# Pair-wise LayerNorm roots, later routing and re-ranked finishing in a two-layer decoder trunk with a gMLP mixer and two MoE stages

## The reference, cut to what matters

```python
for i in range(DEPTH):                                   # DEPTH = 2
    sh_m, sc_m, gt_m, sh_f, sc_f, gt_f = jnp.split(c_act @ ada_w[i] + ada_b[i], 6)
    h = x * (1 + sc_m) + sh_m
    y = sliding_window_attention(h) if i == 0 else chunked_spatial_gating(h)
    x = layer_norm(DEEPNORM_ALPHA * x + (1 + gt_m) * y, post_ln_g[i, 0], post_ln_b[i, 0])
    h = x * (1 + sc_f) + sh_f
    y = hierarchical_moe(h)      # 4 groups x 8 experts, 1 group, 2 experts of it for a token
    x = layer_norm(DEEPNORM_ALPHA * x + (1 + gt_f) * y, post_ln_g[i, 1], post_ln_b[i, 1])

def chunked_spatial_gating(h):                           # chunks of 128 tokens, width 2048
    u, v = jnp.split(gelu(h @ w_in + b_in), 2, axis=-1)
    v = layer_norm(v, sgu_ln_g, sgu_ln_b)
    mixed = einsum(tril(w_s), v) + b_s                   # over the 128 positions of the chunk
    return (u * mixed) @ w_out + b_out
```

## Time and profile before

| | |
|---|---|
| median of 3 runs | 2102.83 us (2079.18, 2102.83, 2133.82) |
| profiled execution | 2081.33 us, span 2080.0 us on core 2, the slowest |
| cores 0 to 3 | 2069.3, 2074.8, 2080.0, 2067.6 us |
| cores 4 to 7 | 2011.6, 2039.3, 2048.1, 2032.3 us |
| TensorE / VectorE / ScalarE / POOL busy | 62 / 54 / 33 / 26 % of the span |
| DMA queues q0 / q1 | 62.6 / 18.2 % of the 16 engines' time |

### The profile page before, as it was taken

One profiled execution on the slowest core, in us unless ns is written; L12 is line 12 of the kernel. 1 busy time (PEld: TensorE's weight loads), 2 busy tenths in 40 slices (PEclk: granted clock), 3 DMA queues, 4 the chain that ended last, 5 costly groups with the idle time before them and its releaser, 6 DMA issues.

```text
span 2080.0 us, 31940 instructions; the slowest of 8 cores (2011.6 to 2080.0 us)
## 1 busy us (share of the span) xinstructions
PE 1296.5 (62%) x9811; PEld 799.6 (38%) x9811; DVE 1127.5 (54%) x2773; ACT 686.5 (33%) x1340; POOL 542.6 (26%) x566
## 2 busy tenths in 40 slices
PE   2569988775067865454517778758868077778430
PEld 1235655442045643232204444445535045545220
DVE  3367766676434422232456786678668633435328
ACT  1135545442034332021203432433332043434135
POOL 2201120211163643333031002011021163546220
PEclk9979999896589988686658898879979588989765
DMA  9986999999269999997866674667659469979976
GB/s 167 178 152 143 161 163 166 144 142 132 102 208 233 170 174 173 168 157 111 197 101 102 121 126 86 116 112 107 116 78 152 142 197 241 267 203 166 170 166 243
DMA packets 93522, 325.09 MB, mean 156 GB/s; under 512 B 27965, under 2 KB 28801, under 8 KB 83608
## 3 DMA queue, kind: packets, MB, share of 16 engines
q0 software_dynamic: 64560, 199.14, 62.6%
q1 hardware_dynamic: 28776, 123.73, 18.2%
HBM read 420.65 MB, written 157.57 MB: 278 GB/s over the span
## 4 chain that ended last, share of the span: by engine, by line
PE 31%; DMA 29%; DVE 15%; issue 15%; ACT 5%; POOL 2%; another core or an unknown queue 2%; DVEq 1%; ACTq 0%; POOLq 0%; SPq 0%
DMA m_XS<-hrow,m_ids 6%; DMA rbuf<-m_ys,m_ids 6%; PE bank L1292 5%; PE bank L1656 5%; DMA rbuf<-n_ys,n_ids 4%; PE bank L1044 3%; PE bank L1727 3%; PE bank L1310 2%; DMA sb_W<-ada_w 2%; PE bank L1133 2%; DMA n_XS<-hrow,n_ids 2%; PE bank L1687 2%; DVE g_nwt L548 2%; PE bank L771 2%
## 5 line engine op out<-in xcount | busy, mean ns | idle before, releaser
L528 POOL DMA_DIRECT2D wbf<-moe_w x108 | 57.0, 528 | 515.2 <-PE bank L1701 162.5
L1292 PE MATMUL bank<-m_hTe,sb_W 128*128 128x256 bf16 x1024 | 147.5, 309 | 55.2 <-DMA sb_W<-moe_w 40.3
L1656 PE MATMUL bank<-sb_W,g_hTg 128*128 128x512 bf16 x512 | 140.9, 425 | 28.0 <-ACT g_hTg L1634 23.9
L1292 PE MATMUL bank<-n_hTe,sb_W 128*128 128x256 bf16 x1024 | 136.6, 295 | 24.8 <-ACT n_hTe L1275 16.6
L1275 ACT ACTIVATE m_hTe<-bank,sb_H_ 128x256 bf16<-128x256 f32 x192 | 94.1, 563 | 166.9 <-PE bank L1268 154.5
L1313 DVE SCALAR_TENSOR_TENSOR m_ys<-bank,m_wv,m_gt 128x512 f32<-128x512 f32 x128 | 88.5, 744 | 106.0 <-DMA rbuf<-m_ys,m_ids 84.4
L1292 PEld LDWEIGHTS bank<-m_hTe,sb_W 128*128 128x128 bf16 x1024 | 111.0, 111 | 88.3 <-issue 62.7
L1275 ACT ACTIVATE n_hTe<-bank,sb_H_ 128x256 bf16<-128x256 f32 x192 | 94.3, 563 | 136.1 <-PE bank L1268 127.5
L1687 PE MATMUL bank<-g_hTg,sb_W 128*128 128x256 bf16 x1024 | 125.5, 279 | 10.7 <-ACT g_uT L1692 10.6
L1318 POOL DMA_INDIRECT rbuf<-m_ys,m_ids x64 | 101.3, 1583 | 101.6 <-DMA rbuf<-m_ys,m_ids 69.4
L1292 PEld LDWEIGHTS bank<-n_hTe,sb_W 128*128 128x128 bf16 x1024 | 106.1, 106 | 50.6 <-issue 30.8
(11 more groups left out here) (343 smaller groups left out, 2669.4 us busy)
## 6 DMA issues: line engine op xcount, KB each, us to landing
wbf<-moe_w POOLq DMA_DIRECT2D x108, 512.0 KB, 12.5
sb_W<-wbf SPq DMA_DIRECT2D x36, 1536.0 KB
sb_W<-moe_w POOLq DMA_DIRECT2D x28, 1536.0 KB, 50.2
sb_W<-ada_w POOLq DMA_DIRECT2D x36, 512.0 KB, 17.4
sb_W<-xin SPq DMA_DIRECT2D x16, 512.0 KB, 14.4
rbuf<-sb_W SPq DMA_DIRECT2D x16, 512.0 KB, 13.5
sb_W<-gmlp_w_in POOLq DMA_DIRECT2D x8, 1024.0 KB, 13.1
g_zt<-rbuf SPq DMA_DIRECT2D x16, 512.0 KB, 12.0
```

The costliest lines, as they stand in the source:

```text
L528: e.dma_start(out=out, in_=in_), reads=reads, writes=writes, adds=adds, proc=proc, after=after)
L1292: S.op("pe", lambda e, f=f, k=k, fb=fb: e.matmul(banks[bk][:, f * 256:(f + 1) * 256], wgu[:, k, fb:fb + 128], hTe[i3][:, k, :], start=(k = ...
L1656: S.op("pe", lambda e, k=k, c=c, bk=bk: e.matmul(banks[bk][:], hTg[:, k, i2 * 128:(i2 + 1) * 128], wvv[:, c, k, :], start=(k == 0), stop=F ...
```

## The change

Seven things, in the order of the diff:
1. The cost table of the scheduler reckons a DMA by its bytes (the larger side; both for `wbf`), at one rate, and an indirect one by its type.
2. `lag` is added to `prio`: 200 for the affines of C, 400 for everything that finishes a gated tile after its roots (m below 7).
3. 26 experts of layer 1 in place of 24 are put into `wbf` ahead of time; the in-phase cast loads of the second MoE go from 6 to 4, its `wbf` loads from 26 to 28.
4. Roots are taken for two tiles at once: `Cpair` (in step 5 of UM) and `finish2`. A pair costs 13 small VectorE instructions of two columns in place of 22 of one. The roots of v stay single.
5. FB stands one pair later, after V and before O, for tiles 2m-4 and 2m-3, with bank 7 for itself; V and O keep banks 0 to 2.
6. In the first iteration both tiles of the first pair take their roots at the start.
7. The output stage has 16 buffers for 16 tiles in place of 8, and issues all loads first.

```diff
         n = free_size(out) * out.shape[0]
-        return ("dma", n * (2 if out.dtype == BF16 else 4), out.dtype != in_.dtype)
+        w = n * (2 if out.dtype == BF16 else 4)
+        r = n * (2 if in_.dtype == BF16 else 4)
+        return ("dma", w + r if out.tensor.name == "wbf" else max(w, r), False)
 
     def indirect_dma_start(self, out=None, out_offset=None, in_=None, in_offset=None, bounds_check=None,
                            oob_is_err=None, compute_op=None):
-        return ("dma", 128 * 4096, True)
...
             if eng == "pool":
                 n.dur *= 2.2
-        n.prio = n.i
+        n.prio = n.i + self.lag
         n.succ = []
         n.left = 0
         self.nodes.append(n)
...
             free[e] = s + n.dur
             if n.dma:
-                rate = 170.0e3 if n.dma[1] else 300.0e3
                 b = max(s + n.dur, dmat[0])
-                dmat[0] = b + n.dma[0] / rate
+                dmat[0] = b + n.dma[0] / 345.0e3
                 n.t1 = dmat[0] + 2.5
             else:
                 n.t1 = free[e]
...
-        pre = [set(range(2, 14)), set(range(2, 26))]
+        pre = [set(range(2, 14)), set(range(2, 28))]
...
-            router(t, hr, bhr)
+        def FB(l, t, pkt, bpkt, hr, bhr, R, use_tanh, ev, pick=None):
+            pick = pick or next_bank
+            transpose_tile(pkt, bpkt, hr, bhr, ev, pick)
+            router(t, hr, bhr, pick)
             if t in batch_end:
                 t0, n = batch_end[t]
-                route_batch(l, t0, n, R, use_tanh, next_bank(), next_bank())
+                route_batch(l, t0, n, R, use_tanh, pick(), next_bank())
                 for q in range(t0, t0 + n):
                     dispatch(l, q)
 
-        gp_[0] = Pool([0, 1, 2, 7])
+        gp_[0] = Pool([0, 1, 2])
+        fbk = Pool([7])
...
+        LAG_C, LAG_O = 200, 400
+
+        def rstd_newton(mean, var, bmv):
             q = nw_i[0] % 4
             nw_i[0] += 1
             w, bw = nwt[q], Bnwt[q]
-            x, y, t, h = w[:, 0:1], w[:, 1:2], w[:, 2:3], w[:, 3:4]
-            ts(x, mv[:, 1:2], LN_EPS, None, ALU.add, None, [bmv], [bw])
+            n = mean.shape[1]
+            x, y, t, h = w[:, 0, 0:n], w[:, 1, 0:n], w[:, 2, 0:n], w[:, 3, 0:n]
+            ts(x, var, LN_EPS, None, ALU.add, None, [bmv], [bw])
             ts(y.bitcast(I32), x.bitcast(I32), 1, None, ALU.logical_shift_right, None, [bw], [bw])
             ts(y.bitcast(I32), y.bitcast(I32), -1.0, RSQ, ALU.mult, ALU.add, [bw], [bw])
-            ts(h, x, -0.5, None, ALU.mult, None, [bw], [bw])
+            if n == 1:
+                ts(h, x, -0.5, None, ALU.mult, None, [bw], [bw])
             for _ in range(3):
-                stt(t, y, h, y, ALU.mult, ALU.mult, [bw], [bw])
+                if n == 1:
+                    stt(t, y, h, y, ALU.mult, ALU.mult, [bw], [bw])
+                else:
+                    tt(t, y, x, ALU.mult, [bw], [bw])
+                    stt(t, t, -0.5, y, ALU.mult, ALU.mult, [bw], [bw])
                 stt(y, t, 1.5, y, ALU.add, ALU.mult, [bw], [bw])
-            stt(x, mv[:, 0:1], -1.0, y, ALU.mult, ALU.mult, [bmv, bw], [bw])
-            return y, bw, x, bw
+            stt(x, mean, -1.0, y, ALU.mult, ALU.mult, [bmv, bw], [bw])
+            return [(y[:, i:i + 1], bw, x[:, i:i + 1], bw) for i in range(n)]
+
+        def pair_stats(k, zs):
+            mvp, bmvp = mvp_[k], Bmvp_[k]
+            for i, (z, bz) in enumerate(zs):
+                si = stats(z, bz)
+                S.op("dve", lambda e, si=si, i=i: e.bn_aggr(out=mvp[:, i, :], in_=st_[si][:]), reads=[Bst_[si]],
+                     **({"writes": [bmvp]} if i == 0 else {"adds": [bmvp]}))
+            r = rstd_newton(mvp[:, :, 0], mvp[:, :, 1], bmvp)
+            return [(mvp[:, i, 0:1], bmvp) + r[i] for i in range(2)]
 
         def load_z(t):
...
-            S.op("act", lambda e: e.activation(out=pkx, in_=z, func=AF.Identity, scale=rs, bias=nm),
-                 reads=[bz, brs, bnm], writes=[Bpkx])
-            affine(z, bz, mv[:, 0:1], bmv, rs, brs, A1, BA1, A0, BA0)
+        def Cpair(m):
+            ts2 = (2 * m, 2 * m + 1)
+            r = pair_stats(m % 2, [(zt[t % NZ], Bzt[t % NZ]) for t in ts2])
+            for t, (mu, bmu, rs, brs, nm, bnm) in zip(ts2, r):
+                z, bz = zt[t % NZ], Bzt[t % NZ]
+                S.op("act", lambda e, t=t, z=z, rs=rs, nm=nm: e.activation(out=pkx_[t % 2], in_=z, func=AF.Identity, scale=rs, bias=nm),
+                     reads=[bz, brs, bnm], writes=[Bpkx_[t % 2]])
+                S.lag = LAG_C
+                affine(z, bz, mu, bmu, rs, brs, A1, BA1, A0, BA0)
+                S.lag = 0
+
+        def finish2(m):
+            ts2 = (2 * m, 2 * m + 1)
+            r = pair_stats(2 + m % 2, [(zt[t % NZ], Bzt[t % NZ]) for t in ts2])
+            S.lag = LAG_O if m < 7 else 0
+            for t, x in zip(ts2, r):
+                finish_apply(t, zt[t % NZ], Bzt[t % NZ], pk[t % 2], Bpk[t % 2], (A3, BA3, A2, BA2), rbuf[1], Br[1], *x)
+                if t + NZ < NT:
+                    load_z(t + NZ)
+            S.lag = 0
 
...
                 V(2 * m + 1)
+            if m >= 2:
+                for t in (2 * m - 4, 2 * m - 3):
+                    FB(1, t, pk[t % 2], Bpk[t % 2], hTr, BhTr, R3, True, ("act", "act"), fbk)
             if m >= 1:
                 for t in (2 * m - 2, 2 * m - 1):
                     O(t)
-                    finish_tile(t, zt[t % NZ], Bzt[t % NZ], pk[t % 2], Bpk[t % 2], (A3, BA3, A2, BA2), rbuf[1], Br[1],
-                                newton=rstd_newton)
-                    if t + NZ < NT:
-                        load_z(t + NZ)
+                finish2(m - 1)
             if m == 7:
                 expert_load(1, 0)
                 expert_load(1, 1)
...
+                    step += 1
                     if m + 1 < 8:
-                        if step == 3:
-                            C(2 * m + 2)
-                        if step == 6:
-                            C(2 * m + 3)
-                    step += 1
+                        if step == 5:
+                            Cpair(m + 1)
             if m == 0:
                 for j in range(16):
                     tt(wov[:, j, :], wov[:, j, :], A2, ALU.mult, [Bwo4[j // 4], BA2], [Bwo4[j // 4]],
...
-            if m >= 1:
-                for t in (2 * m - 2, 2 * m - 1):
-                    FB(1, t, pk[t % 2], Bpk[t % 2], hTr, BhTr, R3, True, ("act", "act"))
             if m + 1 < 8:
                 CB(2 * m + 2)
                 CB(2 * m + 3)
+            if m == 8:
+                for t in (14, 15):
+                    FB(1, t, pk[t % 2], Bpk[t % 2], hTr, BhTr, R3, True, ("act", "act"), next_bank)
         for _ in casts[1]:
             pass
         P3.es.close()
...
-        zo, Bzo = P5.get("zo", [128, D], F32, 8)
+        zo, Bzo = P5.get("zo", [128, D], F32, 16)
         A1, BA1 = P5.get("A1", [128, D])
         A0, BA0 = P5.get("A0", [128, D])
...
```

## The result

The changed kernel takes 2019.78 us (median of 4 runs, 2015.42 to 2024.97), the kernel before 2092.26 (4 runs, 2079.18 to 2133.82). The ratio is 0.9688, 95% interval 0.9634 to 0.9742: **3.1% faster**. Forecast were 2037 us, 1990 to 2088. The profiled execution took 2024.97 us.

What follows compares the result with a forecast made beforehand. gMLP was taken as bound by hand-overs between engines, the MoE stages mostly by transfers. Terms -32 - 8 - 4 - 9 = -53 us on 2081.33 gave 2028; the median, put 9 above, 2037 us, range 1990 to 2088.

Steps and rivals of the forecast that it cites:

- Loop: gMLP pairs 1 to 6, from V of pair 1 to V of pair 7: -35 us.
- These waits are what the later FB moves: End of a gMLP pair: TensorE's waits, 9.8 us, and L722's 8.41 us with routing, go by FB's later place.
- two affines: In the rival where the root ends late: two affines of C now follow the root, 1.3 us each off the pair.
- The pair after the change: gMLP, V to V: 61.6 us without routing in place of 66.4, 69.0 with routing against 73.
- The pair's root eats it: Rival, chance 0.24: in gMLP all 16 evictions follow one late root, V at 67, pairs 2 to 6 only -12, 2060 us.
- Roots at no gain of their own: VectorE in UM: 18 fewer root instructions a pair are nearly free there, so nothing added; 5.0 us if in a chain.
- Pair 0: First gMLP pair: -8 of the 9.0 us that TensorE waited for `g_pkx`, between 0 and -9.
- Ahead of the second MoE: `n_ids` no longer waits for its table, which SP now loads first: -3.7 us, between 0 and -3.7.
- Second MoE: Two casts become `wbf` loads and save 9.4 us of transfer: -9 us, between 0 and -19.
- First MoE: Gathers and scatters alternate evenly, nothing added or removed: 0, between -10 and +10 us.
- Slower by bank 7: Rival, chance 0.12: FB's one bank exposes hand-overs, 8.4 us a pair, and L724 waits 8.4 us: +84, 2121 us.
- Output: Output stage: 16 buffers move loads earlier but no instruction, costed at nothing, -2 to +1 us.

Runs made afterwards that it cites:

- experiment 3, FB old: Changed kernel with FB back in its old place and both lags at 0: 2034.75 us, ratio 0.9795 to the kernel before.
- experiment 5: Changed kernel with a root of one column for each tile: 2010.61 us; the same with FB in its old place: 2007.28 us, ratio 0.9654.
- experiment 4: Changed kernel with FB back in its old place and the four banks shared again: 2013.93 us, ratio 0.9689 to the kernel before.

## Why the prediction was right, and where it was not

- **Loop, -35 forecast, -33 measured: right in size, wrong in cause.** The step that failed is "These waits are what the later FB moves". It holds for the wait for routing (39.0 to 1.9 us on core 0) and fails for the logits': without the lag, FB's later place leaves 23.7 of 29.8 us. The runs put in its place: the lag 15.5 us (experiment 3, FB old), the rest (roots, C in step 5, table, not told apart) 8.4 (419.7 to 411.3), FB's move 9.4, which the tail gives back in the mean (10.0 gained on die 0, 10.8 lost on die 1). I costed the lag at nothing, by leaving it out of the sum; it stood only in a rival, as two affines. That the sum of the pairs came out at -33 is luck.
- **The pair after the change, 61.6 and 69.0 us.** 61 and 68.3 on die 0, some 75 on die 1, by stops that no row of mine foretold. "The pair's root eats it" falls: V came at 61, not 67.
- **Roots at no gain of their own: right** (experiment 5). The choice between the row's 0.28 us and the 61 ns of the Trainium skill ("VectorE: DVE Perf Modes", section "The TRN2 errata") decided nothing: these instructions lay on no path that sets the end. The same section says that this row of its table predicts too little, and that the measured fixed term is some 150 cycles; single ones of one column lasted 0.14 to 0.21 us in the trace of before, which agrees with that (157 ns) and not with 61 ns.
- **Pair 0, -8: wrong, +9.5.** The 9.0 us of waits for `g_pkx` did go, as forecast, and pair 0 grew by 9.5 all the same, by something I had no term for. The suspect of the prediction, "the multiplication of w_out's rows, now ahead of V's statistics, may delay them", is not it: that stop costs 45 us, but in either kernel, and with it gone from both the 8.8 us stay. A wait of 7.1 us for w_in, new in the changed kernel, may be a part. The cause stays open. The larger miss is that the row for the 45 us was in the trace of before: 29.8 us of VectorE's wait for w_out.
- **Ahead of the second MoE, -3.7: right** (0.17 in place of 3.74 us of wait). The tail's +3.8 is routing in pair 7: in the loop's account it was to be +3, and experiment 4 has near 10.
- **Second MoE, -9: mis-sized, -31.6.** The two experts gave 7.6 of it as forecast; the cost table 20, and more in the changed kernel (40 us between 342.5 and 302.0). **First MoE, 0: -11**, just past the bound of 10 that I gave; the table alone has -14.7. I costed a part of the change that orders the MoE stages' queue at nothing, because it changes neither bytes nor instructions there.
- **Slower by bank 7: out.** L724 waits 0.95 us, the waits among FB's pieces are 0.8 us each.
- **Output, -2 to +1: +1.4**, no gain from 16 buffers.

The errors of +17.5 us in pair 0 and -34 in the MoE stages partly cancelled, and the longest core stood on another die than before, so that the sum of 2028 on the profiled execution's scale met 2025 by luck as much as by reckoning.

## What to carry to other kernels

Where a list scheduler writes the queues, its cost of a transfer is a part of the kernel: ask for each engine which instruction it puts ahead of work that is ready, and look in the trace for the longest wait of an engine on a DMA whose result nobody needs yet. A wait's releaser says what came last, not which move removes it: the wait for the logits went for the most part by ranking other work on VectorE later, with the router left in place. A longer stage is not explained by the largest stop in it, when the kernel before has the same stop: take it out of both and compare. And a stretch that pays (the loop) must be read with the one behind it (the tail), or moved work counts as saved.

## What the runs showed of the hardware

- The longer die is not always the same: attention took 572.6 and 556.2 us on dies 0 and 1 in the profile of before, 556.2 and 571.0 in that of the changed kernel, and die 1 was the longer in all 12 profiles of the experiments. Whether that goes with the execution or with the chip is not shown. A comparison of the slowest cores of two executions can compare two dies.
- In pairs with routing all of die 1 lost 5 to 7 us a pair, on core 5 in a stop of VectorE and ScalarE together (6.28 and 6.95 us), beside 8 scatters of POOL; with FB in the old place, where the scatters fall elsewhere, the dies differ by 1 us in such a pair. It is not bound to die 1: with single roots cores 2 and 3 stopped for 6.2 and 5.2 us in pair 7. Nor to FB's new place: in the kernel before with the cost table ScalarE of core 4 stopped for 6.8 us in pair 3. In these cases the stop began 5.6 us (core 5), 6.4 (core 2) and 6.5 (core 4) behind the first of the 8 scatters; scatters without a stop are as common. Whether the scatters, the fetching of instructions or another core's transfers hold the engines was not tried and stays open.
